# A 64-row product that nothing reads, put behind four spreads and transposes of a two-block network on one core

## The reference

```python
# first block, layer 0: gated recurrence; layer 1: sparse attention; after each an MLP
for layer in range(2):
    hn = rms_norm(x, norm_mix_g[layer])
    mix = rglru_mixer(hn, ...) if layer == 0 else dsa_mixer(hn, ...)
    x = x + mix
    x = x + square(relu(rms_norm(x, norm_mlp_g[layer]) @ mlp_w_up[layer])) @ mlp_w_down[layer]
x = rms_norm(x, final_norm_g)
# second block
h  = rms_norm_2(x,   norm_g) * (1 + scale)   + shift      # scale, shift, gate from c @ w_ada
hc = rms_norm_2(ctx, norm_g) * (1 + scale_c) + shift_c
z  = h @ w_in                                             # 1024 -> 8704
k, v   = per-head rms_norm of z's key columns, z's value columns; kc, vc the same from hc
ya = neighbourhood_attention(q, k, v, kc, vc, rpb) * silu(z_a)
yb = short convolution branch; yc = convolution of 31 taps, layer norm, silu
x  = x + gate * ((ga * (ya @ w_out_a) + gb * (yb @ w_out_b) + gc * (yc @ w_out_c)) @ w_o)
```

## Time and profile before

| | us |
|---|---|
| median of 3 runs | 882.61 |
| the runs | 882.99, 877.87, 882.61 |
| the profiled execution, its time | 882.57 |
| its span, first to last instruction | 880.8 |
| TensorE busy | 872.7 (99% of the span) |
| VectorE, ScalarE, GpSimd busy | 656.7, 499.8, 46.5 |

### The profile page before, as it was taken

How to read it: one execution, slowest core, us unless ns; L and a number is a source line. 1 busy time by engine, 2 the same in 40 slices (tenths; PEclk the granted TensorE clock), 3 DMA queues, 4 the chain that set the end, 5 groups by cost and what they waited for, 6 DMA issues and landing times.

```text
span 880.8 us, 17592 instructions
## 1 busy us (share of the span) xinstructions
PE 872.7 (99%) x7192; PEld 848.5 (96%) x7192; DVE 656.7 (75%) x1261; ACT 499.8 (57%) x907; POOL 46.5 (5%) x62
## 2 busy tenths in 40 slices
PE   9999999999999999999999999999999999999998
PEld 8988999999999888999999999999999999999998
DVE  6878668898877785676577555565898888897873
ACT  5696777764435656668777444344545554545550
POOL 0000000000000054000000000021020000000000
PEclk9999999999999999999999999999999999999999
DMA  9917778878978461167757855518455222465541
GB/s 304 336 50 239 242 221 264 270 266 273 304 251 287 153 192 49 49 218 229 213 160 219 239 176 178 182 44 210 150 165 171 96 74 72 149 212 177 177 150 49
DMA packets 162817, 164.23 MB, mean 186 GB/s; under 512 B 16768, under 2 KB 159280, under 8 KB 162480
## 3 DMA queue, kind: packets, MB, share of 16 engines
q1 hardware_dynamic: 162736, 163.10, 58.6%
HBM read 162.01 MB, written 2.91 MB: 187 GB/s over the span
## 4 chain that ended last, share of the span: by engine, by line
PE 93%; DVE 2%; ACT 2%; issue 1%; DMA 1%; POOL 0%; SPq 0%; DVEq 0%
PE ps L316 24%; PE ps L318 23%; PE ps L320 23%; PE ps L1522 2%; PE ps L1520 2%; PE ps L1524 2%; PE ps L1579 2%; PE ps L1089 2%; PE ps L439 1%; PE ps L1614 1%; PE ps L1618 1%; PE ps L1616 1%; PE ps L456 1%; PE ps L1570 1%; PE ps L1561 1%
## 5 line engine op out<-in xcount | busy, mean ns | idle before, releaser
L283 DVE TENSOR_TENSOR wl<-raw,wh 128x1024 fp32r<-128x1024 f32 x256 | 308.3, 1221 | 31.9 <-ACT wh L276 31.9
L316 PE MATMUL ps<-xh,wh 128*128 128x256 f32 x1136 | 320.3, 282 | 0.0
L318 PE MATMUL ps<-xl,wh 128*128 128x256 f32 x1136 | 315.6, 278 | 0.1
L320 PE MATMUL ps<-xh,wl 128*128 128x256 f32 x1136 | 315.6, 278 | 0.0
L276 ACT ACTIVATE wh<-raw 128x1024 fp32r<-128x1024 f32 x256 | 266.6, 1050 | 73.0 <-PE ps L320 66.1
L316 PEld LDWEIGHTS ps<-xh,wh 128*128 128x128 f32 x1136 | 213.8, 188 | 2.9 <-issue 1.7
L318 PEld LDWEIGHTS ps<-xl,wh 128*128 128x128 f32 x1136 | 214.2, 189 | 0.5 <-DVE xl L384 0.3
L320 PEld LDWEIGHTS ps<-xh,wl 128*128 128x128 f32 x1136 | 213.5, 188 | 0.0
L316 PE MATMUL ps<-hh,wh 128*128 128x256 f32 x512 | 142.6, 278 | 0.0
L318 PE MATMUL ps<-hl,wh 128*128 128x256 f32 x512 | 142.6, 278 | 0.0
L320 PE MATMUL ps<-hh,wl 128*128 128x256 f32 x512 | 142.6, 278 | 0.0
(11 more groups left out here) (359 smaller groups left out, 1454.9 us busy)
## 6 DMA issues: line engine op xcount, KB each, us to landing
raw<-in_w_in_dram SPq DMA_DIRECT2D x34, 1024.0 KB, 5.3
raw<-in_mlp_up_dram SPq DMA_DIRECT2D x32, 1024.0 KB, 5.5
raw<-in_mlp_down_dram SPq DMA_DIRECT2D x32, 1024.0 KB, 7.1
aw<-in_w_adaT_dram SPq DMA_DIRECT2D x24, 512.0 KB, 4.7
raw<-in_rec_w_in_dram SPq DMA_DIRECT2D x7, 1024.0 KB, 10.8
raw<-in_att_w_in_dram SPq DMA_DIRECT2D x6, 1024.0 KB, 6.1
raw<-in_rec_w_out_dram SPq DMA_DIRECT2D x4, 1024.0 KB, 6.9
raw<-in_att_w_o_dram SPq DMA_DIRECT2D x4, 1024.0 KB, 5.0
```

Source lines behind the costliest of these rows:

```text
L283: e.tensor_tensor(parts_of(i)[1], raw_of(i), f32(parts_of(i)[0]), op=ALU.subtract).then_inc(S["wl"], 1)
L316: e.matmul(o, H[:, first + n], xh[:, k], start=start and n == 0, stop=False)
L318: e.matmul(o, H[:, first + n], xl[:, k], start=False, stop=False)
L320: ins = e.matmul(o, L[:, first + n], xh[:, k], start=False, stop=stop and n == len(ks) - 1)
```

## The change

A helper `half_rows` issues one fp32 matmul: 64 rows of `NEGH`, broadcast to 64x128, are stationary, 64 rows of it broadcast to 256 columns move; the result goes to the bank `AUX[0]`, and nothing reads it. It is called behind the spread at f = 1 in both MLPs, behind the spread at f = 16 in the second, and behind `tensor_turn(3)`. Nothing is removed or moved.

```diff
+
+    def half_rows(e, q):
+
+        e.matmul(claim(q, AUX[0])[:, 0:256], NEGH[0:64, 0:1].to_broadcast([64, 128]),
+                 NEGH[0:64, 0:1].to_broadcast([64, 256]), start=True, stop=True)
...
             if f == 1:
                 rms_spread_pe(e, q, 1 + 2 * l)
+                half_rows(e, q)
             if l and f == 15:
                 rms_sum_pe(e, q, 4)
             if l and f == 16:
                 rms_spread_pe(e, q, 4)
+                half_rows(e, q)
...
         tensor_values2(e, q, 1)
         tensor_turn(e, q, 3)
+        half_rows(e, q)
         tensor_values2(e, q, 2)
```

## The result

The changed kernel takes 891.14 us (median of 20 executions, 881.75 to 893.39) against 882.13 of before in the same comparison (20 executions, 877.29 to 884.53): a ratio of 1.0089, interval 1.0071 to 1.0106. It is slower, and it lies above the range that was given (877.5 to 886.5). The profiled execution took 891.49 us, its span 889.7.

The account below looks back on a forecast made before the run. TensorE, busy 872.7 of 880.8 us, was taken to bound the kernel. 882.57 + 3.2 for four half-row products - 4.8 for the faster pace at Site C = 881.0 us; range 877.5 to 886.5.

Parts of the forecast that it names:

- two paces: TensorE runs the same tile product at about 113.7 or 117.8 ns, without idle time and at the same clock.
- a pace, once entered, lasts: On TensorE, the pace set at a stretch's entry was said to hold for hundreds of products.
- D: Behind `tensor_turn(3)` at 603 us: gain 0, bound 1.6 us, cost 0.8 us; `tensor_rows` seemed to have no fast pace.
- The price of a half-row product: Each added 64-row fp32 product costs TensorE 0.81 us, 3.2 us for four; bounds 1.7 to 4.2 us for four.
- Site A: Behind the spread at f = 1 of the first MLP, 106 us: 1512 products already fast; gain 0, cost 0.8 us.
- Rival 3: First MLP's f = 1 stretch turns slow, costing 6.2 us, while second MLP's f = 16 stretch turns fast: 887.2 us, chance 0.10.
- Site C: Behind the spread at f = 16 of the second MLP, 432 us: 1128 products turn fast; gain 4.8, cost 0.8 us.
- The seven of eight: Tile products directly behind 64-row products in the trace: seven of eight entries settled at the fast pace, 276 ns records.
- B: Behind the spread at f = 1 of the second MLP, 390 us: 336 products already fast; gain 0, cost 0.8 us.
- Rival 4: The 256-column fp32 stream sets the slow pace behind all three spreads: 893.5 us, +1.2%, chance 0.06.
- rival 1: No memory of the entry, or the second MLP's f = 16 stretch stays at 117.8 ns: 885.8 us, chance 0.18.
- Slower by over 1%: Whole kernel slower than 891.4 us, given chance 0.05.

Follow-up runs that it names:

- experiments on entries: Four kernels with small fp32 products added behind nearly all rows of both MLPs of the kernel before; the pace of following rows was read, no time given.

## Why the prediction was wrong, point by point

**What bounds the kernel, and two paces.** Held, but for "a pace, once entered, lasts": behind D it turned within a row of products, with no job between. TensorE's records and the lengths of stretches gave both paces, and every large difference in these runs is a stretch that changed from one to the other.

**The price of a half-row product.** Held: 0.81 us predicted, 0.8 measured, from the three rows it was made of.

**Site A, "Gain 0, cost 0.8".** This is the step that failed. It took A's fast pace as given because the trace of before showed it. It was the work of the spread, which turns the slow second row into a fast third, in all profiles. Behind spread and half-row product the outcome hangs on a row further back, slow in 12 of 17 profiles: 6.4 us for 1512 products in the profiled execution. Rival 3 named this with 6.2 us and a chance of 0.10.

**Site C, gain 4.8.** Failed as well. C stayed slow in the profile and in all twelve executions with the product at C alone. The place of the spread behind its wait, which the prediction noted and left ("stays"), was the handle; whether the wait itself or the one row more is what tells isn't separated. The size was about right: with the spread moved the kernel gained 5.6 us (882.47 to 876.89), the 0.25 us of idle time and 48 products of `tensor_rows` included.

**The seven of eight.** Here both steps have their root. Entries were counted by what stood directly before and not by the pace before that. In the experiments on entries a spread, the half-row product and both together turn the pace, and at A even the pace before doesn't settle what both together do; a count that ignores the state before them says little about an entry.

**B and D.** Right in size: B stayed fast, and in the profile of the change D gained nothing. D's reason was wrong: `tensor_rows` can run fast, and in the profile of B and D alone 288 products behind the first 96 did, 1.1 us less for the whole stretch, though not by the product at D.

**The rivals.** Rival 4 came nearest in time, 893.5 against 891.1, but not in mechanism: it wanted A and B slow by the fp32 stream, and B was fast. What happened is rival 3 at A with rival 1 at C, 882.57 + 3.2 + 6.2 = 892.0, a combination that was given no chance. "Slower by over 1%" had 0.05; the ratio is 1.0089, its interval on both sides of that line.

The Trainium skill's warm gap of N / 2.4 + 2.5 ns ("TensorE: Matmul & The Clock Gate", "Back-to-back issue gap"), 109 ns here, knows no state; the section calls it the gap of an isolated matmul and says that in a stream both the weight loads and the matmuls set the spacing. By the formula the change would have cost 3.2 us, and it cost 9.0; in the trace the same product at the same clock starts every 113 or 118 ns for a whole stretch.

**What stays open.** Why there are two paces, what the state behind them is (two rows that look alike can answer differently to the same sum), and what leaves the mixer's output, and by it the first row, at one pace in one execution and at the other in the next. That the first row sets A is shown; by what path, two rows on, is not. Open too is whether C needs the wait gone or the second row.

## What to carry to other kernels

A long row of equal matmuls can have two steady paces, here 4% apart, and small jobs between rows may turn one into the other. Before adding an instruction to fix a pace, count its outcomes by the state that it meets, not only by what stands directly before. A product in front of a stretch that is fast already can only lose it. Where a small job sits behind a wait, first try to move it to where its operand is ready: here that move alone gave 0.7% on the chip where C was slow in all executions of before, and needed no added work.

## What the runs showed of the hardware that was not expected

- Two fp32 products of 128 columns between rows of fp32r products, issued without a wait, turned the pace of the next row in 52 of 52 cases of the two kernels that had them: 113 to 118 ns and back.
- One fp32 product of 128 rows and 256 columns alone was followed by the fast pace in 26 of 26, one of 64 rows by the opposite pace in 26 of 26.
- A load of 64 rows and the first load of 128 rows behind it start with their matmul and not 0.11 us ahead. The half-row product, with both changes, costs 0.8 us where its streaming is 0.43, so the two changes cost some 0.4 us.
- In all 17 profiles in which nothing was added ahead of it, the first row of the first MLP ran at the opposite pace to the 192 products before the fp32 product over 32 rows that parts them.
